# A decoder block with 32 streamed experts: the break in the expert loop moved from expert 15 to expert 5, w_ple and p loaded ahead of the ring, 28 products at the start of TensorE

## The reference

```
x = x + merged @ w_out                       # after two attention branches
x = x + moe_ffn(rmsnorm(x, g_ffn), w_router, b_router, w_e1, b_e1, w_e2, b_e2)
x = x + sigmoid(rmsnorm(x, g_ple) @ w_ple_gate) * (p @ w_ple)

moe_ffn: top 4 of 32 experts per token, softmax over the four;
  gu = xe @ w1[e] + b1[e]                    # 1024 -> 2048
  act = (clip(lin) + 1) * gate * sigmoid(1.702 * gate)
  y = act @ w2[e] + b2[e]                    # 1024 -> 1024, added with its weight
```

## Time and profile before

| | |
|---|---|
| median of 3 runs | 1221.12 us (1220.26 to 1221.61) |
| the profiled execution's own time | 1221.16 us |
| its span, first to last instruction | 1219.0 us |
| TensorE busy | 1149.2 us (94%) |
| VectorE, ScalarE, GpSimd busy | 272.3, 191.7, 34.8 us |
| transfers | 448.39 MB, mean 368 GB/s |
| experts, from the first gather | 276 to 1184 us |

### The profile page before, as it was taken

How to read it: one execution, slowest core, us unless ns; L and a number is a source line. 1 busy time by engine, 2 the same in 40 slices (tenths; PEclk the granted TensorE clock), 3 DMA queues, 4 the chain that set the end, 5 groups by cost and what they waited for, 6 DMA issues and landing times.

```text
span 1219.0 us, 15142 instructions
## 1 busy us (share of the span) xinstructions
PE 1149.2 (94%) x6374; PEld 489.3 (40%) x6374; DVE 272.3 (22%) x784; ACT 191.7 (16%) x407; POOL 34.8 (3%) x49
## 2 busy tenths in 40 slices
PE   7999999999999999999989789999989898988998
PEld 4455544454333343333333333333333343333344
DVE  1474543253111121111111111111112111111112
ACT  1223445131111111111111100000000000000011
POOL 2122100000000000000000000000000000000000
PEclk9999999999999999999999989999999999999999
DMA  8934170979999999999999999999999999999990
GB/s 273 343 139 158 50 208 31 419 243 380 421 430 432 430 432 431 430 434 432 430 432 430 426 430 432 430 431 433 431 431 433 431 431 432 431 432 432 425 378 34
DMA packets 40315, 448.39 MB, mean 368 GB/s; under 512 B 7455, under 2 KB 10624, under 8 KB 26354
## 3 DMA queue, kind: packets, MB, share of 16 engines
q1 hardware_dynamic: 38686, 441.66, 86.8%
q0 software_dynamic: 1264, 5.27, 1.2%
q10 hardware_dynamic: 324, 0.86, 0.3%
HBM read 446.71 MB, written 4.22 MB: 370 GB/s over the span
## 4 chain that ended last, share of the span: by engine, by line
PE 69%; DMA 28%; ACT 1%; issue 1%; DVE 0%; ACTq 0%; DVEq 0%
PE ps L435 22%; DMA wbuf<-in_w_e 16%; PE ps L464 13%; DMA ring<-in_w_e 12%; PE ps L1531 7%; PE ps L1614 5%; PE ps L407 4%; PE ps L398 3%; PE ps L1737 2%; PE ps L1647 2%; PE ps L1668 2%; PE ps L1578 2%; ACT xres L584 1%; PE ps L454 1%; PE ps L1605 1%
## 5 line engine op out<-in xcount | busy, mean ns | idle before, releaser
L435 PE MATMUL ps<-ring,xres 128*64 128x512 f32 x1216 | 277.0, 611 | 17.7 <-DMA ring<-in_w_e 17.5
L435 PE MATMUL ps<-wbuf,xres 128*64 128x512 f32 x832 | 186.2, 602 | 9.6 <-DMA wbuf<-in_w_e 9.6
L647 DVE TENSOR_SCALAR oT<-ps 128x512 f32<-128x512 f32 x32 | 22.1, 692 | 703.3 <-PE ps L435 703.3
L435 PEld LDWEIGHTS ps<-ring,xres 128*64 128x64 f32 x1216 | 88.9, 141 | 194.5 <-issue 165.3
L464 PE MATMUL ps<-ring,xres 128*64 128x512 f32 x608 | 134.8, 595 | 12.5 <-ACT xres L584 12.5
L435 PEld LDWEIGHTS ps<-wbuf,xres 128*64 128x64 f32 x832 | 60.5, 138 | 127.7 <-issue 110.2
L464 PE MATMUL ps<-wbuf,xres 128*64 128x512 f32 x384 | 85.0, 595 | 8.1 <-ACT xres L584 8.1
L580 ACT ACTIVATE oT<-oT 128x512 f32<-128x512 f32 x30 | 18.9, 630 | 451.1 <-DVE oT L647 451.1
L1531 PE MATMUL ps<-wbuf,hT 128*128 128x512 f32 (+2 forms) x224 | 86.1, 542 | 0.0
L464 PEld LDWEIGHTS ps<-ring,xres 128*64 128x64 f32 x608 | 42.2, 137 | 91.8 <-issue 80.5
L407 PE MATMUL ps<-xres 64*128 64x512 f32 x256 | 63.6, 615 | 0.0
(11 more groups left out here) (251 smaller groups left out, 789.9 us busy)
## 6 DMA issues: line engine op xcount, KB each, us to landing
ring<-in_w_e SPq DMA_DIRECT2D x50, 4096.0 KB, 37.1
wbuf<-in_w_e SPq DMA_DIRECT2D x34, 4096.0 KB, 37.8
ring<-in_w_e SPq DMA_DIRECT2D x16, 2048.0 KB, 24.0
wbuf<-in_w_in SPq DMA_DIRECT2D x9, 2048.0 KB, 12.7
wbuf<-in_w_e SPq DMA_DIRECT2D x8, 2048.0 KB, 9.8
wbuf<-in_w_out SPq DMA_DIRECT2D x2, 2048.0 KB, 8.4
wbuf<-in_w_ple_gate SPq DMA_DIRECT2D x2, 2048.0 KB, 41.1
rel_rows_repeated<-rel_rows POOLq DMA_DIRECT2D x1, 3072.0 KB, 20.4
```

The costliest lines, as they stand in the source:

```text
L435: l = mm((G, Lb)[n // 2][(n % 2) * SLOTS:(n % 2 + 1) * SLOTS, :], xeT[:, k, :], dealt(slots[at][:, r * 2 * DFF:(r + 1) * 2 * DFF])[n], sta ...
L647: d.tensor_scalar(gc, ps[0][:, :], LIMIT, None, ALU.min).then_inc(s["gc_ready"], 1)
```

## The change

- PLE_AFTER is 5. The break stands after the five visits that are written out, followed by one loop over 25 experts and `last_pair`. All of this, with the last stage (the gate products), is a function `remaining`, which stands once in the arm of the usual path (`n_max <= SLOTS`), straight behind the branch, and a second time behind the general path in the Else arm.
- w_ple goes to hT, issued as the first router product is done; p goes over the places of gqk and wr, issued as both are done. The ring has no foreign slots any more; `position` and `uses` are gone.
- The fourth PLE product goes to bank 2. The four copies wait until all products are done, two on ScalarE, two on VectorE. TensorE waits for them behind the branch.
- GATE_SLOTS, x3 and x3T lie in other slots.
- 28 products of 64 by 64 outputs stand ahead of TensorE's first wait for the constants.

```diff
-PLE_AFTER = 15
+PLE_AFTER = 5
-GATE_SLOTS = [(NE * PIECES + 2 + i) % NS for i in range(2)]
+GATE_SLOTS = [(NE * PIECES + i) % NS for i in range(2)]
+WARM = 28
...
-        ple_slot = Take(slots[PLE_AT % NS])
-        wple, pin, pT = ple_slot(2, DM), ple_slot(TT, PLE), ple_slot(2, SEQ)
+        p_words = misc[:, 569:1081]
+        pin, pT = p_words.rearrange("p (t d) -> p t d", t=TT), p_words.rearrange("p (k t) -> p k t", k=2)
+        wple = hT[:, :].rearrange("p (k n) -> p k n", k=2)
...
-        x3T = ring[:, 0:KT * SEQ].rearrange("p (k t) -> p k t", k=KT)
+        x3T = slots[8][:, 0:KT * SEQ].rearrange("p (k t) -> p k t", k=KT)
...
-        def position(n):
-            return n if n < PLE_AT else n + 2
-        def uses(pos):
-            return pos // NS + 1 - (pos >= PLE_AT and pos % NS // 2 == PLE_AT % NS // 2)
...
-        def expert_pe(te, a):
+        def expert_pe(te, a, finish=None):
...
                 te.wait_ge(b1_cast, 2)
-                def five(g, late):
-                    for j in range(ROUND):
-                        visit(g * ROUND + j, lambda i: place(g, j, i, late))
-
-                for j in range(ROUND):
+                for j in range(PLE_AFTER):
                     visit(j, lambda i: place_of(j * PIECES + i), j == 0)
-                with te.Fori(1, PLE_AFTER // ROUND) as g:
-                    five(g, 0)
                 ple_pe(te)
+
+                def remaining():
+                    with te.Fori(PLE_AFTER // ROUND, PAIR // ROUND) as g:
+                        for j in range(ROUND):
+                            visit(g * ROUND + j, lambda i: place(g, j, i))
+                    last_pair(PAIR, lambda i: place_of(PAIR * PIECES + i))
+                    finish()
+
                 n_max = largest(te)
-                with te.If(n_max > SLOTS):
+                with te.If(n_max <= SLOTS):
+                    te.wait_ge(pl_ev, 3)
+                    te.wait_ge(pl_right, 2)
+                    remaining()
+                with te.Else():
+                    te.wait_ge(pl_ev, 3)
+                    te.wait_ge(pl_right, 2)
                     scatter_of(PLE_AFTER - 1).then_inc(flushed, 1)
                     expert_pe(te, rest)
-                with te.Fori(PLE_AFTER // ROUND, PAIR // ROUND) as g:
-                    five(g, 1)
-                last_pair(PAIR, lambda i: place_of(PAIR * PIECES + i))
+                    remaining()
...
             for i in range(4):
                 t, n = i // 2, (i % 2) * 512
                 if i == 3:
-                    te.wait_ge(pl_ev, 1)
+                    te.wait_ge(first["s"]["out_ready"], PLE_AFTER + 1)
                 for k in range(2):
-                    l = mm(ps[(0, 1, 3, 0)[i]][:, :], pT[:, k, t * P:(t + 1) * P], wple[:, k, n:n + 512], start=k == 0, stop=k == 1)
+                    l = mm(ps[(0, 1, 3, 2)[i]][:, :], pT[:, k, t * P:(t + 1) * P], wple[:, k, n:n + 512], start=k == 0, stop=k == 1)
                 l.then_inc(pl_ps, 1)
-            te.wait_ge(pl_ev, 4)
 
         def ple_act(sc):
-            sc.wait_ge(pt_ps, 1)
-            nc.scalar.copy(pT, ps[3][:, :].rearrange("p (k t) -> p k t", k=2)).then_inc(pt_ev, 1)
-            for i in range(4):
-                sc.wait_ge(pl_ps, i + 1)
-                nc.scalar.copy(pl[:, i // 2, (i % 2) * 512:(i % 2 + 1) * 512], ps[(0, 1, 3, 0)[i]][:, :]).then_inc(pl_ev, 1)
+            sc.wait_ge(pl_ps, 1)
+            nc.scalar.copy(pT, ps[3][:, :].rearrange("p (k t) -> p k t", k=2)).then_inc(pl_ev, 1)
+            sc.wait_ge(pl_ps, 5)
+            for i in (0, 2):
+                nc.scalar.copy(pl[:, i // 2, 0:512], ps[(0, 3)[i // 2]][:, :]).then_inc(pl_ev, 1)
+
+        def ple_dve(ve):
+            ve.wait_ge(pl_ps, 5)
+            for i in (1, 3):
+                nc.vector.tensor_copy(pl[:, i // 2, 512:1024], ps[(1, 2)[i // 2]][:, :]).then_inc(pl_right, 1)
...
                 load_first(sp, 7)
+                sp.wait_ge(rt_ps, 1)
+                sp.dma_start(wple, io["w_ple"][0].rearrange("(k p) n -> p k n", p=P)).then_inc(ld_ple, 16)
                 sp.wait_ge(x2_taken, 1)
...
                 sp.wait_ge(rt_ps, 2)
+                sp.dma_start(pin, io["p"][0, 0].rearrange("(t p) d -> p t d", p=P)).then_inc(ld_p, 16)
                 sp.wait_ge(hp_ready, 4)
                 load_first(sp, 9)
...
                     if n == PLE_AT:
-                        sp.wait_ge(used, PLE_AT - NS + 1)
-                        sp.dma_start(wple, io["w_ple"][0].rearrange("(k p) n -> p k n", p=P)).then_inc(ld_ple, 16)
-                        sp.dma_start(pin, io["p"][0, 0].rearrange("(t p) d -> p t d", p=P)).then_inc(ld_p, 16)
                         n_max = largest(sp)
...
+                te.wait_ge(pool_ch, 1)
+                for _ in range(WARM):
+                    mm(ps[7][0:SLOTS, 0:64], half, half, start=True, stop=True)
                 te.wait_ge(ld_const, 16 * 4)
```

More of the change, by code:

```diff
@@ L239, in block_kernel @@
         wple_g = [slots[i].rearrange("p (k n) -> p k n", k=4) for i in GATE_SLOTS]
-        ple_slot = Take(slots[PLE_AT % NS])
-        wple, pin, pT = ple_slot(2, DM), ple_slot(TT, PLE), ple_slot(2, SEQ)
+        p_words = misc[:, 569:1081]
+        assert gqk.shape[1] * gqk.shape[2] + wr.shape[1] * wr.shape[2] == TT * PLE
+        pin, pT = p_words.rearrange("p (t d) -> p t d", t=TT), p_words.rearrange("p (k t) -> p k t", k=2)
+        wple = hT[:, :].rearrange("p (k n) -> p k n", k=2)
         v = Take(xres)
@@ L258, in block_kernel @@
         pl = hT[:, :].rearrange("p (t d) -> p t d", t=TT)
-        x3T = ring[:, 0:KT * SEQ].rearrange("p (k t) -> p k t", k=KT)
+        x3T = slots[8][:, 0:KT * SEQ].rearrange("p (k t) -> p k t", k=KT)
         v = Take(slots[6])
         wST_last, actT_last, oe_last = v(TT * P), v(4, P), v(512)
-        x3 = ring[:, KT * SEQ:KT * SEQ + TT * DM].rearrange("p (t d) -> p t d", t=TT)
+        x3 = slots[8][:, KT * SEQ:KT * SEQ + TT * DM].rearrange("p (t d) -> p t d", t=TT)
         xn3, sgate = xn, sq
@@ L323, in block_kernel, with place @@
         rest = dict(s=expert_sems("b"), piece=[sem(f"piece_b{i}") for i in range(PIECES)], col=NE, visits=(ROUNDS - 1) * NE, pre=0)
-        def position(n):
-            return n if n < PLE_AT else n + 2
-        def uses(pos):
-            return pos // NS + 1 - (pos >= PLE_AT and pos % NS // 2 == PLE_AT % NS // 2)
-        def place(g, j, i, late):
-            at = PIECES * j + i + 2 * late
-            pair = at % NS // 2
+        def place(g, j, i):
+            at = PIECES * j + i
             if at % 2:
                 return at % NS, None, 0
-            first_uses = 1 - (late and pair == PLE_AT % NS // 2)
-            return at % NS, piece[pair], g * (16 * ROUND * PIECES // NS) + 16 * (at // NS + first_uses)
+            return at % NS, piece[at % NS // 2], g * (16 * ROUND * PIECES // NS) + 16 * (at // NS + 1)
         def place_of(n):
[L344 to L347, removed]
+            pair = n % NS // 2
+            if n % 2 == 0:
+                return n % NS, piece[pair], 16 * (n // NS + 1)
             if n in WHOLE:
-                return pos % NS, None, 0
-            halves = [q for q in range(n + 1) if q not in WHOLE and position(q) % NS == pos % NS]
-            return pos % NS, piece[PAIRS + pair], 16 * len(halves)
+                return n % NS, None, 0
+            halves = [q for q in range(n + 1) if q not in WHOLE and q % NS == n % NS]
+            return n % NS, piece[PAIRS + pair], 16 * len(halves)
         def load(eng, e, i, at, signal):
@@ L364, in load_whole @@
             e, i = IN_ORDER[n]
-            pair = position(n) % NS // 2
+            pair = n % NS // 2
             src = w1[e, i // 2] if i < UP else w2[e]
@@ L369, in load_first @@
         def load_first(eng, n):
-            slot = position(n) % NS
+            slot = n % NS
             load(eng, *IN_ORDER[n], slot, piece[slot // 2 + PAIRS * (slot % 2)])
@@ L666, in expert_dve @@
                     visit(it)
+                ple_dve(ve)
                 n_max = largest(ve)
@@ L776, in _ @@
                     last = n + (n in WHOLE)
[L777 to L781, removed]
+                    sp.wait_ge(used, last - NS + 1)
                     if n in WHOLE:
@@ L787, in _ @@
                 for i in range(2):
-                    sp.wait_ge(used, position(NE * PIECES) + i - NS - 1)
+                    sp.wait_ge(used, NE * PIECES + i - NS + 1)
                     sp.dma_start(wple_g[i], w_gate[:, 4 * i:4 * i + 4]).then_inc(ld_ple_gate[i], 16)
@@ L1720, in _ @@
                 take_x2(te, 1, 0)
-                expert_pe(te, first)
                 def x3_rows(t, m_):
@@ L1738, in gate, with last_stage @@
                     l.then_inc(g_ps, 1)
[L1740 to L1746, removed]
+                def last_stage():
+                    x3_rows(0, 0)
+                    x3_rows(0, 1)
+                    x3_rows(1, 0)
+                    gate(0)
+                    x3_rows(1, 1)
```

(3 more changed lines are left out.)

7 lines of the change are left out of this document (3 added, 4 removed).

## The result

The changed kernel takes 1215.14 us (median of 6; 1214.58 to 1216.80) against 1220.76 us of the kernel before (median of 6 beside it). The ratio is 0.9948, interval 0.9935 to 0.9962: faster by 0.52%, which is 6.3 us; by the medians it is 5.6 us. 4.7 were forecast. Run again later, it took 1215.45 us against 1220.83, ratio 0.9953 (0.9940 to 0.9966). The forecast of 1216.5 had the direction, and the range began at 1215.4, 0.3 us too high. The profiled execution took 1216.80 us.

A forecast was written before the change was run, and what follows sets the result against it. The prediction took the weight stream as the bound from about expert 10 to 30. From 1221.16 us it took 3.2 for w_ple and p and 1.5 for the warm-up, giving 1216.5 us; range 1215.4 to 1221.5.

The forecast's parts named there:

- The bound: From about expert 10 to expert 30, how early the weight stream runs sets the end time; loads hold about 430 GB/s.
- w_ple and p out of the ring: Both loads move from ahead of expert 15 into a 3.3 us gap ahead of piece 9: gain 3.2 us.
- The stop: TensorE's pause at the break, now at expert 5: 10.0 us, with the branch taken as hidden behind the copies.
- The cover: At expert 5 the queued weight loads bear a TensorE stop of up to 11.9 us without a gap.
- Rival C: Branch at expert 5 stalls as before: 18.2 us against 11.9 of cover, stream loses 6.3 us, 1222.8 us; chance 0.12.
- The longer loop ...: 0: The longer loop and ScalarE's and VectorE's branches cost 0, hidden behind expert 5's up product.
- The warm start: 28 products ahead of TensorE's first wait make the first transposes run at full rate: gain 1.5 us, bounds 0 and 1.8.
- Landed 8.4 us later, at 10.2: The first projection's weights, issued at 1.78, land at 10.2 against its start at 11.70, which limits the early gain to 1.5 us.
- The doubt about the granted-clock column: At 8 to 9 us the column reads 1.00 where the transposes' durations say half; one of the two is wrong.
- Rival B: The warm-up doesn't raise the rate, or its gain is lost in the attention stage: 1218.0 us; chance 0.15.
- Rival D: TensorE's jump over the second arm at the end stalls 8.07 us behind the last product: 1220.9 us; chance 0.10.
- Rival E: w_ple and p aren't absorbed in the gap ahead of piece 9: 1219.7 us; chance 0.08.

The follow-up runs named there:

- experiment 6: Changed kernel with only the early loads of w_ple and p kept: no products at the start, break at expert 15, two loops, old layout; 1218.39 us.
- experiment 5: Kernel before with the 28 products put at its start, its two loops kept; 1224.78 us against 1221.62 us for the kernel before.
- 9: Changed kernel with 18 small products on TensorE ahead of its wait for expert 30's third piece; 1215.69 us, ratio 0.9947 to the kernel before.
- experiment 8: Changed kernel with 4 unread products of 512 columns behind the break, and 24 products at the start for 28; 1216.23 us.
- experiment 3: Changed kernel with its one loop of 25 experts split into two loops of 10 and 15; 1216.76 us, ratio 0.9970 to the kernel before.
- experiment 2: Changed kernel with its 28 first products cut to one column each; 1217.11 us, ratio 0.9965 to the kernel before.
- 11: Changed kernel with one residual product moved behind the rank products and 9 small products ahead of the wait for expert 30's third piece; 1216.66 us.

## Why the prediction was right and wrong

**The bound** held: all transfers together run at 423 GB/s and more from the 11th slice to the 38th, and TensorE's last wait ends 0.04 us behind a transfer.

**w_ple and p out of the ring**, 3.2 us: right. Piece 9 landed at 284.8, not later than before, and the step of 3.3 us in the stream is gone, here and in experiment 6. The gap was less free than I read it, and something behind it takes up the rest: with piece 9 issued at 274.7 and 274.6, it lands at 282.0 without the early loads (experiment 5) and at 284.9 with them (9), yet load 17 lands at 325.1 and 325.0.

**The stop**, 10.0 us and nothing for the branch: 10.1 in the trace. **The cover**, 11.9 us: with a stop of 10.1 + 3.4 = 13.5 us the stream was 1.4 us late, where 13.5 - 11.9 = 1.6 were due (experiment 8). Rival C was right as a mechanism; the one size off is the stop with the jump, reckoned at 16.5 us and 1.7 of low clock. It was 428.29 - 410.26 = 18.0 us, and load 29 went out 2.2 us later behind it than in changed, so 8.4 us are lost and not 6.3. What decided against it was the layout.

**"The longer loop ...: 0"** is the step that failed. I reckoned the loop in TensorE's time alone, where a back edge costs nothing, and it doesn't. But two loops are two bodies of code, and the code comes in transfers, which the page counts on the same 16 engines as the weights. Eight packets of it, about one pass of a body, cost the stream 1.5 us in a place where every microsecond counts. The kernel before had a second pass behind the break; the changed one doesn't (11 packets for 19 in the full stream), and experiment 3 gives the 1.5 us back by splitting the loop. With this term the forecast would have been 1216.5 - 1.5 = 1215.0, for 1215.14 and 1215.45 measured.

**The warm start**, 1.5 us: 1 to 2 by experiment 2, so the size can't be called wrong. "Landed 8.4 us later, at 10.2" was: the first weights landed at 9.62 in the changed kernel, and its chain gained 2.1 us at the start. The doubt about the granted-clock column went the other way: it reads 1.00 at 8 to 9 us before and after, while the transposes take 3.67 and 1.97 us. The durations were right. Rival B is out for most executions and not for all: of the ten profiles with products of 64 columns ahead, eight have the transposes at 1.97 us, and those of experiments 8 and 11 have them at 3.58 and 3.43.

**Rival D**, the jump at the end: no cost. The execution takes 2.2 us more than its span, as before. **Rival E** is out: nothing of piece 9's delay is left at load 17.

Sum: 3.2 + 1.5 + 1.5 = 6.2 us with the forecast's two sizes and the missing one, and 5.4 to 6.3 are measured. What moves single executions is the clock: it falls behind TensorE's last wait in both profiles of the changed kernel and not in the one of before (1.7 us), and in one of them at 271 (1.5 us). The fall at the last wait comes with a wait of 2.5 us: experiments 3 and 8, with nearly the same kernel, end with waits of 1.00 and 0.83 us and no fall. How often it falls without the profiler isn't shown.

The Trainium skill (Runtime: NRT & Kernel Launch, "Instruction fetch mechanics") says that the sequencer brings code in blocks of 256 instructions by its own DMA queue, mostly hidden. By the trace it is hidden for TensorE in the changed kernel, where no idle time of the products is put down to "issue", less so with 63 packets (9.5 us), and not for a weight stream that fills the transfer engines.

## What to carry to other kernels

Where a full stream of transfers sets the time, count the code as a part of it: read the instruction queue's packets in the profile, and write a long loop once. After any edit ahead of a long loop read that count again: 28 products decided over 36 packets and 7 us here. A stop of the consuming engine was free up to the depth of the queue at that place, the time to landing less one load: 21.8 - 9.7 = 12.1 us at expert 5, where 10.1 cost nothing and 13.5 cost 1.4.

## What the runs showed that was not expected

- A packet of code costs the weight stream about 0.2 us on average: 7, 29 and 36 more of them cost 1.3 to 1.6, 4.2 to 5.2 and 6.9 us. The cost comes as one step of 1.5 us in eight packets.
- Whether a loop of 25 experts is loaded once or in each round hung on 28 products ahead of it: 27 packets with them, of whatever work, and 63 without; in the kernel before it was the other way round, 32 without and 61 with them.
- 28 products with one column each held TensorE for 6.1 us, more than the 5.0 us of those with 64 (4.9 to 6.0 in the profiles with all 28), and left the transposes at half rate.
- The granted clock fell to 0.50 within 271 to 276 with TensorE busy throughout, in two of 14 profiles.
- Late in the changed kernel TensorE's waits for the stream alternate between 2.5 us with a low clock behind and 0.8 without, and the kind that comes last is worth 1.7 us.
